# VectorE adds the squares for seven norms down to one tile less, TensorE sums one tile less

## What is computed

```python
def rms_norm(x, g):
    xf = x.astype(jnp.float32)
    y = xf * lax.rsqrt(jnp.mean(xf * xf, axis=-1, keepdims=True) + RMS_EPS)
    return (y * g.astype(jnp.float32)).astype(x.dtype)
...
    h = rms_norm(x, ffn_norm_g[l])
    x = x + conv_glu_ffn(h, w_up[l], ffn_conv_w[l], w_down[l])
    return rms_norm(x, final_norm_g)
...
    kv = rmsnorm(h, kv_norm) @ w_kv
    proj = rmsnorm(h, norm_mix[l]) @ w_in[l]
    mkv = rmsnorm(mem, mem_norm[l]) @ w_mem_kv[l]
    h = h + sq_relu_mlp(rmsnorm(h, norm_mlp[l]), w_up[l], w_down[l])
```

## Time and profile before

| | |
|---|---|
| median of 3 runs | 1028.47 us |
| the three runs | 1026.59, 1028.47, 1029.01 us |
| span of the profiled execution | 1024.5 us, 4.0 us under the median |
| TensorE busy (matmuls) | 998.7 us, 97% |
| TensorE weight loads | 967.2 us, 94% |
| VectorE busy | 698.6 us, 68% |
| ScalarE busy | 546.2 us, 53% |
| mean share of the 16 DMA engines | about 46% by the weight queue |

### The profile page before, as it was taken

One profiled execution on the slowest core, in us unless ns is written; L12 is line 12 of the kernel. 1 busy time (PEld: TensorE's weight loads), 2 busy tenths in 40 slices (PEclk: granted clock), 3 DMA queues, 4 the chain that ended last, 5 costly groups with the idle time before them and its releaser, 6 DMA issues.

```text
span 1024.5 us, 20191 instructions
## 1 busy us (share of the span) xinstructions
PE 998.7 (97%) x8416; PEld 967.2 (94%) x8416; DVE 698.6 (68%) x863; ACT 546.2 (53%) x707; POOL 40.8 (4%) x26
## 2 busy tenths in 40 slices
PE   6999999999999999998999999999999999999998
PEld 5998898998999999998988999999999999999998
DVE  5678754653878888899894755556786867555553
ACT  5556556553675555465653544344486665444442
POOL 0034121000000000000000000000000000000000
PEclk9999999999999999999999999999999999999999
DMA  7643333333554655545333364565543234556451
GB/s 277 230 176 115 137 121 101 111 119 123 191 198 158 225 206 169 201 165 206 124 117 125 133 242 164 205 205 169 205 158 109 101 124 170 201 195 208 170 205 42
DMA packets 24832, 169.12 MB, mean 165 GB/s; under 512 B 2752, under 2 KB 3264, under 8 KB 4800
## 3 DMA queue, kind: packets, MB, share of 16 engines
q1 hardware_dynamic: 24192, 165.98, 46.3%
q10 hardware_dynamic: 576, 2.20, 0.6%
HBM read 167.12 MB, written 1.05 MB: 164 GB/s over the span
## 4 chain that ended last, share of the span: by engine, by line
PE 80%; DVE 13%; ACT 5%; issue 2%; DMA 0%; DVEq 0%; ACTq 0%
PE G L590 13%; PE G L591 13%; PE G L592 13%; PE D L590 8%; PE D L592 8%; PE D L591 8%; DVE wlo L1765 4%; PE M L590 2%; PE M L592 2%; PE M L591 2%; ACT whi L1248 2%; PE M L827 1%; PE D L841 1%; PE D L1149 1%; PE D L1176 1%
## 5 line engine op out<-in xcount | busy, mean ns | idle before, releaser
L1765 DVE TENSOR_TENSOR wlo<-raw,whi 128x2048 fp32r<-128x2048 f32 x155 | 354.1, 2290 | 122.5 <-ACT whi L1248 122.3
L590 PE MATMUL G<-xh,whi 128*128 128x256 f32 x1280 | 361.7, 283 | 4.2 <-DVE xl L1786 2.9
L592 PE MATMUL G<-xh,wlo 128*128 128x256 f32 x1280 | 355.0, 277 | 0.0
L591 PE MATMUL G<-xl,whi 128*128 128x256 f32 x1280 | 355.0, 277 | 0.0
L1248 ACT ACTIVATE whi<-raw 128x2048 fp32r<-128x2048 f32 x155 | 295.6, 1910 | 50.3 <-PE D L592 47.2
L590 PEld LDWEIGHTS G<-xh,whi 128*128 128x128 f32 x1280 | 241.1, 188 | 11.1 <-DVE wlo L1765 6.5
L591 PEld LDWEIGHTS G<-xl,whi 128*128 128x128 f32 x1280 | 240.6, 188 | 1.3 <-issue 1.2
L592 PEld LDWEIGHTS G<-xh,wlo 128*128 128x128 f32 x1280 | 240.7, 188 | 0.0
L590 PE MATMUL D<-hh,whi 128*128 128x256 f32 x672 | 185.8, 276 | 0.8 <-issue 0.8
L591 PE MATMUL D<-hl,whi 128*128 128x256 f32 x672 | 185.6, 276 | 0.0
L592 PE MATMUL D<-hh,wlo 128*128 128x256 f32 x672 | 185.6, 276 | 0.0
(11 more groups left out here) (385 smaller groups left out, 1432.2 us busy)
## 6 DMA issues: line engine op xcount, KB each, us to landing
raw<-wall_dram SPq DMA_DIRECT2D x155, 1024.0 KB, 4.9
x<-x_dram SPq DMA_DIRECT2D x4, 256.0 KB, 5.2
mem<-mem_dram ACTq DMA_DIRECT2D x1, 1024.0 KB, 4.7
out_dram<-x SPq DMA_DIRECT2D x4, 256.0 KB, 2.3
poolw<-pool_w_dram ACTq DMA_DIRECT2D x1, 768.0 KB, 6.3
cst<-cst_dram SPq DMA_DIRECT2D x1, 448.0 KB, 12.0
lora<-lora_dram SPq DMA_DIRECT2D x1, 256.0 KB, 11.5
sgw<-sg_w_dram SPq DMA_DIRECT2D x1, 256.0 KB, 12.2
```

Of the source, the lines that this page charges most:

```text
L590: mm(out, w_h, hi, start=start, stop=False, skip_group_check=skip)
L591: mm(out, w_h, lo, start=False, stop=False, skip_group_check=skip)
L592: return mm(out, w_l, hi, start=False, stop=stop, skip_group_check=skip)
L1765: signal(tt(wlo[:, pan.slot, 0:w], raw[:, pan.slot, 0:w], f32(whi[:, pan.slot, 0:w]), SUB), "w_lo")
```

## The change

After the last wide add, VectorE waits for it and adds the second tile onto the first (128x256), and signals after that. TensorE multiplies one tile by ones where it had two, three where it had four (norm 1), and one column per half of the positions where it had two (norms 3 and 5). The memory sum is included, since it uses the same helpers.

```diff
         def summed(out, buf, sem, before):
 
             pe.wait_ge(S(sem), before + 1)
-            for k in (0, 1):
-                ins = mm(out, ones, buf[:, k, :], start=k == 0, stop=k == 1)
-            return ins
+            return mm(out, ones, buf[:, 0, :])
...
                 pe.wait_ge(S("sq_sum"), 1)
                 pe.wait_ge(S("sq"), 8)
-                for k in (0, 1, 6, 7):
+                for k in (0, 6, 7):
                     ins = mm(M[1][:, 0, :], ones, wk2[:, k, :], start=k == 0, stop=k == 7)
...
                 for b in range(2):
-                    for k in (0, 1):
-                        ins = mm(DB[3][:, 0, b:b + 1], wk2[:, k, b * P:(b + 1) * P], ones[:, 0:1], start=k == 0, stop=k == 1)
+                    ins = mm(DB[3][:, 0, b:b + 1], wk2[:, 0, b * P:(b + 1) * P], ones[:, 0:1])
...
             ins = tt(buf[:, 0:2, :], buf[:, 0:2, :], buf[:, 2 * i:2 * i + 2, :], ADD)
-            if i < last:
-                own(ins)
-            else:
-                signal(ins, done)
+            own(ins)
+            if i == last:
+                signal(tt(buf[:, 0, :], buf[:, 0, :], buf[:, 1, :], ADD), done)
```

## The result

| | before | after |
|---|---|---|
| median, first session (4 runs each) | 1027.53 us (1026.36 to 1029.01) | 1033.67 us (1033.42 to 1035.74) |
| span of the profiled execution | 1024.5 us | 1032.0 us |
| ratio, with its 95% interval | | 1.006 (1.0045 to 1.0076) |

The changed kernel is 0.6% slower, where 1029.5 us and no measurable change were forecast. The time lies outside the range, and past rival 2, which was the slow side.

What follows compares the result with a forecast made beforehand. TensorE was busy 97% of the span, with VectorE's chain deciding at most sums. Of 3.8 us taken from TensorE little comes out, six of seven adds do: +1.0 us on the median 1028.47, 1029.5 us, range 1026.4 to 1031.9.

Steps and rivals of the forecast that it cites:

- rival 2: TensorE's clock falls after new gaps before 299.8 and 509.7 us: 1032.2 us at the scores; chance there or both 0.13.
- memory and norm 1: Two adds push the last `xl` by 0.90 us, one matmul saved after it: +0.47 us, carried on.
- norm 2: Restart after the sum at +0.92 us, less a saved matmul of 0.43: shift from +0.47 to +0.49.
- norm 3: VectorE's chain from the adds to scores L1105 takes the add, TensorE's 0.83 us saving only waits: +0.45 us.
- norm 5: The add fits a 0.48 us wait for ScalarE, and both TensorE savings come out: -0.83 us.
- The add: At each sum, last wide and narrow add together cost VectorE 0.45 us more, bounds 0.35 and 0.55.
- the forecast's aside: By the Trainium skill's table (0.33 us an add), each add costs 0.1 us less and the sum is 0.5 lower.
- Norms 4 and 6: Behind these sums the saved matmul ends in the wait for `wlo`, the add comes out in full: +0.45 us each.
- Rival 1: TensorE bounds everywhere, all adds lie beside other work, 3.8 us come out: 1024.7 us; chance 0.09, middle case 1027.7, 0.12.
- rival 3: Low clock stretch at 534.7 us vanishes or doubles: 1027.8 us (0.08) or 1031.2 (within 0.10 for a single extra stretch).
- The base: Sum added to span 1024.5 gives 1025.5 us; on median 1028.47, with the same 4.0 around it, 1029.5 us.

Runs made afterwards that it cites:

- Either part of the change alone: Kernel before with the change for memory sum and norms 1 to 5 only, or norm 6 only: 1027.55 us (0.994) and 1028.17 us (0.9946).
- filling the waits: Four 512-column products with `xh` weights behind norm 4's and 6's sums: kernel before 1028.59 us, with norm 5's change 1027.12, changed kernel (more products) 1031.39.
- the pin: Kernel before plus two unread 512-column products in the panel behind norm 4's and 6's sums: 1027.54 us, on another chip 1034.05; changed kernel so 1028.26.

## Why the prediction was wrong, step by step

This is how much the shift between the two matched traces grew at each place (us), beside the forecast. What the shift did between these places is left out; up to 852 us it comes to +0.3 us:

| | forecast | measured |
|---|---|---|
| memory and norm 1 (1.72 to 2.16) | +0.47 | +0.44 |
| norm 2, with the saved product at its full-clock price | +0.02 | +0.04 |
| norm 3 (0.89 to 1.35) | +0.45 | +0.46 |
| norm 4 (1.17 to 1.63) | +0.45 | +0.46 |
| norm 5 (1.59 to 0.71) | -0.83 | -0.88 |
| norm 6 (0.80 to 1.26) | +0.45 | +0.46 |
| sum | +1.0 | +0.98 |

So every term that the forecast had came out. What it lacked is the rest of the 7.5 us.

- **The add, 0.45 us for the last wide and the narrow one: right.** The six narrow adds take 424 to 426 ns in the kernel after, as the row of another add of that shape had it:

```profile
L1818 DVE TENSOR_TENSOR wk<-wk x6: 424/426/426, 298.5 to 849.4; 128x256 f32<-128x256 f32 x6
L1818 DVE TENSOR_TENSOR mwk<-mwk x1: 425/425/425, 291.9 to 291.9; 128x256 f32<-128x256 f32 x1
```

  The Trainium skill (VectorE: DVE Perf Modes, The TRN2 errata) has, beside the table that gave an estimate of 0.33 us, a formula for an f32 add, (elements + 151) cycles at 0.96 GHz, which by an estimate gives 424 ns here. The trace agrees with the formula and not with the table. (By the table six adds of 0.1 us less would make 0.6 us, not the 0.5 of the forecast's aside.)
- **Memory and norm 1, +0.47: right.** VectorE's shift grows by 0.46 us at each of the two adds, from 1.72 to 2.64, and one matmul saved at norm 1 leaves 2.21; from 400 to 480 us it is 2.16. The gap before the last quarter is there, charged to `xl` with 1.06 us idle, 1.34 us from start to start. It is smaller than the 1.5 forecast because TensorE came to it later: its shift had grown from 1.73 to 2.22 us before the memory sum without a wait, at a slower spacing of its matmuls.
- **Norm 2, +0.02 or 0: the restart right, what follows a draw of the clock.** The restart came 0.47 us later (the sum waited 4.2 us). Then the low stretch was 3.4 us long where it had been 6.8 in the kernel before, and the shift fell by 1.75 us, from 2.63 to 0.88. The saved product is 0.43 of that, and the clock the other 1.3. This is nearly what the kernel after had lost at 242 us, ahead of all that the change touches, where its clock was down for 3.4 us and the shift rose by 1.5. 241 to 248 us of the kernel after (busy us (x) of each engine, granted clock):

```profile
241.00:248.00 7.00, 7.00 (x44) 6.67 (x44) 0.00 (x0) 2.44 (x4) 0.00 (x0) 0.76 0.01 2
```

  Of 18 profiles 10 have such a stretch there, with and without the change. That these two draws nearly cancelled is why the shift at 852 us looks like the forecast's sum to 0.3 us.
- **Norm 3, +0.45: right.** VectorE's shift goes from 0.89 to 1.35 at the adds, and L1102 waits 1.8 us. "About 1.5" was forecast; TensorE's own work there was early, with a shift of -0.34.
- **Norms 4 and 6, +0.45 each: the waits right, the price far off.** From the last record of the sum to the panel's first it is 1.26 us from start to start where it was 0.37, for both (1.28 forecast). Less the product saved that makes +0.46 each: the sum of norm 6 starts 0.80 us later than in the kernel before, the panel behind it 1.26 us. What was wrong is what the sum did with these waits. It took a restart to cost its lateness and nothing else.
- **Norm 5, -0.83: right.** The shift falls from 1.59 us at the sum to 0.71 at `rstd`. The chain has one product of two records and four columns:

```profile
754.56 0.43 PE M L634 x2
754.99 0.35 PE D L653 x4
755.37 0.48 ACT rstd L1231
```
- **The step that failed** is the one that the sum never had: that TensorE's work in the loops has one price. All terms were waits and removed instructions, and the 8394 records left were carried on at their old durations. The missing term is 6.2 us for a slow part. It is larger than all that the change touches together.
- **The rivals.** Rival 1 falls with the waits for `wlo` behind norms 4 and 6, which grew to 0.89 us. Rival 2 said that the change makes gaps, and that TensorE may be slower after them. That was near, but its places were not: in the kernel after the clock stayed at 1.00 behind both of its gaps (297.5 to 301.5 and 507 to 511 us), and the loss lies behind norm 6's wait. The granted clock was also the wrong thing to watch: it is 1.00 through all the slow loops. The low clock at the scores cost 1.1 us in one profile. For rival 3, the low stretch at 534.7 moved to 535.6, and the shift changed by 0.2 us there, not 1.7.
- **The base.** The forecast added 4.0 us around the span. The kernel after's profiled execution took 1033.82 us for a span of 1032.0, so 1.8 us lie around it, and the other 2.2 us were, by an estimate from that, the distance of the profiled execution of before from the median. With a kernel whose runs fall in groups 6 us apart, a median of three runs says which group two of them fell in. The range should have been drawn from that: on the chips of the experiments the kernel before alone ran from 1023.8 to 1043.0 us.

**What is shown, and what isn't.** Shown: the two paces and their price; that the 6.2 us of the first comparison are the slow pace in the last feed-forward part; that a loop without a wait keeps its pace to the end; and what a long product does to the pace. The runs' groups go with it in the main: the profiled executions with no slow part have spans from 1023.3 to 1029.6 us, those with one from 1028.8 to 1036.3 and those with two 1035.1 and 1038.6. Shown by counts: the changed kernel falls into the upper groups more often than the kernel before. In the three sessions that had both, 22 of its 28 runs lie over 1031 us against 28 of 74, and its median is 4.7 and 4.2 us longer on the two chips where both had many runs. On the chip where the changed kernel was not run, the kernel before had 23 of 31 there, as full a share. Not settled: why. Either part of the change alone left the slow groups nearly empty, and so did filling the waits in the kernels without the whole change, but not in the changed kernel. So it isn't one wait of the change that does it. That its extra waits do it together, as more restarts ahead of long loops, fits this and isn't shown. What in a restart sets the pace stays open, and so does whether the chip has a part in it.

## What to carry to other kernels

A kernel that is bound by one engine for a thousand microseconds has a second term beside its waits: what one instruction of the long loops costs. Compare the count of instructions in a window in the middle of each loop, before and after, ahead of any talk of waits; a difference of 4% in a loop that the edit doesn't touch is larger than most edits. And if repeated runs of one kernel fall into groups, compare the groups and how full they are, not a median of four, and on more than one chip: the pin looked perfect on the first and failed on the second.

## What the runs showed of the hardware

- With a weight load for each matmul of 256 columns, TensorE started one every 113.3 ns or every 117.8 ns at the full granted clock, for up to 1409 in a row, and in the slow loops the load of one in three took 192 ns instead of 188. The Trainium skill (TensorE: Matmul & The Clock Gate, Wait — 56ns, not 53.3ns?) gives one time from start to start for warm matmuls back to back, the columns at 2.4 GHz and about 2.5 ns, by which an estimate for 256 columns is 109.2 ns. The trace shows neither of its paces so low.
- In the feed-forward loops the pace outlasted everything but a wait (two starts 0.13 us apart instead of 0.11 were enough) or a product of 512 columns with `whi` as weights. In each of the 138 such products, the load that was slow ahead of it decided the pace behind it. In the mixer of the first block the pace also changed without either, at about 126 and 220 us in all 18 profiles.
- The granted clock was low for stretches of 3.4 or 6.8 us that differ between executions. The kernel before with the pin had one from 484.4 to 491.2 us in one profile, and in the other none there but one from 508.9 to 512.3. The stretch at 242 us cost 1.5 us in the kernel after, so two profiles of one kernel can differ by more than the sum that this forecast was about.
